# Attention scores of a hybrid mixer: 288 rows of high and low parts in two full passes and one on row quarters

## The chip, the cores and the metric

One Trainium2 chip, one of its NeuronCores. The metric is the device time of one execution in microseconds. A change is compared by the median of repeated runs. All arithmetic that counts is float32; products that must be nearly exact in float32 are made from a high part (the value rounded to the float32r type) and a low part (value minus high part), as high x high + high x low + low x high.

## What is computed

A transformer layer over 2048 tokens (x) and 256 context tokens, width 1024, in the order of the reference:

```
h, hc = modulated rmsnorm of x, ctx
cq, ckv, kr, rq, rk, rv, rg = split(h @ w_in)
q = (rmsnorm(cq) @ w_uq)      8 heads x (64 plain + 32 rope)
k, v = rmsnorm(ckv) @ w_ukv   8 heads x 64; the 32 rope rows of k are shared by all heads
s = q . k * 96**-0.5 ; p = softmax(s over 2304 keys) ; o = p @ v
y = [o, bidirectional retention of rq, rk, rv gated by rg] @ w_o
x = x + ga1 * y ; then a 16-expert feed-forward on the normed x, and a final rmsnorm
```

The change is about s, the scores: 2048 queries x 2304 keys x 8 heads over 96 rows (64 plain, 32 rope).

## The kernel before, in words

The program runs stages one after the other, each in a block of its own with all five engines in step by semaphores. Every engine executes its own instruction list in order; `sg[name].wait(engine, turn, k)` makes it wait for the k-th increment of that turn.

**project** (18 turns of 128 tokens). TensorE multiplies the normed tokens by w_in in high and low parts (L501), transposes the latents (L526), and makes q (L542), k (L548), v (L554), the chunk state (L560) and q transposed per head (L568). VectorE does norms, the sums of the rest of the modulation (L723), rope for the retention keys (L707 to L714), h^T (L692, L694), latent_T (L764) and the rope rows of the attention key, kr_T (L765); TensorE's L542 waits for the last increment of `latT`, which L765 gives. At the end of its turn VectorE waits for ScalarE's statistics (L586). SyncE stores k, q, kr and the rest to scratch in device memory, in a fixed order (L418).

**retention** (16 chunks). Among others the 128 x 128 scores of eight heads are made by L968 on 64 rows of the array each: four heads on rows 0 to 63, then four heads on rows 64 to 127.

**attention** (L1178 to L1462), the stage that the change rewrites. The work is 32 blocks: 8 heads x 4 blocks of 512 queries. SyncE loads a head's k^T and q^T (96 rows: 64 plain, 32 rope) two heads ahead; ScalarE rounds them (L1355) and VectorE subtracts (L1394), in thirds between blocks. For every key tile of 128 keys (18 of them) three passes of 96 rows and 512 columns add into one of four PSUM banks:

```
for n, (kp, qp) in enumerate(((0, 0), (0, 1), (1, 0))):
    m = pe.matmul(banks[S_BANKS[kt % 4]][:, :], kT[u][:, kp, k], qT[u][:, qp, q], ...)
```

A turn of TensorE is: all 54 score passes of block b+1, then six groups of `weighted` of block b (three key tiles each: values times probabilities on 64-column halves of the array, L1315, and the sums of the probabilities on 32-column quarters, L1319), with the transposes that find the maximum of block b+1 between them (`max_rows` L1297 after group 2, `max_spread` L1305 after group 4). ScalarE copies each score tile out of PSUM (L1360, 512 columns each) and takes the exponentials of three tiles at a time (L1365). VectorE takes the maximum over keys (L1402, L1405, L1411, L1416, L1418), subtracts it (`shift`, L1424), inverts the sums (L1430) and multiplies the outputs by the inverse (L1435, eight small instructions), before SyncE stores them to `attT`.

**mix_out** (16 tiles of 128 tokens): loads the attention output (L1521), ScalarE rounds it (L1628), GpSimd takes the low part (L1560), TensorE multiplies by w_o (L1585), VectorE adds, norms and routes. **experts** follows and is not changed but for the semaphores that it takes over.

## Time and profile before

| | us |
|---|---|
| median of 3 runs (2973.39 to 2991.9) | 2974.0 |
| the profiled execution, its own time | 2979.84 |
| its span in the trace | 2978.0 |
| TensorE matmul busy, of the span | 2749.8 (92%) |
| VectorE busy | 2099.8 (71%) |
| ScalarE busy | 1441.5 (48%) |
| GpSimd busy | 348.9 (12%) |
| the L1285 score passes, busy | 413.9 |

Durations below are of the one profiled execution. In its rows a group has its busy time, its count and the mean of one instruction; matmuls overlap in the pipeline, so the mean of one (400 ns for a score pass) is longer than the distance from one to the next. A time of one step is therefore taken from the start of a group of instructions to the start of the next one. In the trace a matmul on plain float32 operands appears as two instructions, one on float32r as one. "PEld" is the load of the stationary operand, which stands in the trace as an engine of its own.

### The profile page before, as it was taken

How to read it: one execution, taken by the hardware profiler on the slowest of the kernel's cores; microseconds unless marked ns; L12 is line 12 of the kernel's file. 1: busy time of each engine (PE TensorE's matmuls, PEld its weight loads, DVE VectorE, ACT ScalarE, POOL GpSimd, SP SyncE). 2: the span in 40 equal slices, each digit the busy share in tenths (PEclk: the TensorE clock that was granted, in tenths of full speed). 3: DMA queues.
4: the chain of work that ended last, by engine and by line, in shares of the span. 5: the costliest groups of instructions: out<-in, count | busy, mean ns of one | idle time of the engine just before them, and what ended most of it. 6: DMA issues, size and time to landing. Idle time of an engine off the chain costs nothing. (4 is left out here: it accounts for less than half of the span.)

```text
span 2978.0 us, 57085 instructions
## 1 busy us (share of the span) xinstructions
PE 2749.8 (92%) x20805; PEld 2244.1 (75%) x20805; DVE 2099.8 (71%) x3131; ACT 1441.5 (48%) x2146; POOL 348.9 (12%) x377
## 2 busy tenths in 40 slices
PE   5999999899959999999999979992999999999996
PEld 2877777688847766766766748882989988988995
DVE  3555554677749999999999965547667667657666
ACT  3555555322237767767766742112444444444444
POOL 0111111222210000000000002210101101101102
PEclk8999999999979999999999989995999999999998
DMA  7544443422230110110110024334667767767778
GB/s 244 176 158 151 149 149 113 134 76 76 62 61 3 37 33 10 37 32 11 37 34 10 5 85 153 134 116 132 206 191 226 225 190 207 226 179 219 226 217 306
DMA packets 267042, 375.33 MB, mean 126 GB/s; under 512 B 35571, under 2 KB 186646, under 8 KB 265174
## 3 DMA queue, kind: packets, MB, share of 16 engines
q1 hardware_dynamic: 257334, 337.83, 35.5%
q0 software_dynamic: 9504, 34.61, 5.0%
q8 instruction: 150, 2.46, 0.4%
q14 instruction: 54, 0.44, 0.1%
HBM read 286.61 MB, written 85.77 MB: 125 GB/s over the span
## 5 line engine op out<-in xcount | busy, mean ns | idle before, releaser
L2012 PE MATMUL ebank<-gathered_T,w_gate_up 128*128 128x256 f32 x4608 | 552.5, 282 | 20.8 <-issue 13.8
L2012 PEld LDWEIGHTS ebank<-gathered_T,w_gate_up 128*128 128x128 f32 x4608 | 548.3, 190 | 24.3 <-issue 23.4
L1285 PE MATMUL abank<-head_qT,head_kT 96*128 96x512 f32 x1728 | 413.9, 400 | 22.8 <-DVE head_qT L1394 17.0
L1285 PEld LDWEIGHTS abank<-head_qT,head_kT 96*128 96x128 f32 x1728 | 325.6, 191 | 104.2 <-issue 29.3
L1365 ACT ACTIVATE scores<-scores 128x1536 f32<-128x1536 f32 x192 | 274.3, 1476 | 232.9 <-DVE scores L1424 232.9
L1424 DVE TENSOR_TENSOR scores<-scores,abank 128x1536 f32<-128x1536 f32 x192 | 322.6, 1747 | 47.9 <-PE abank L1305 44.8
L1360 ACT ACTIVATE scores<-abank 128x512 f32<-128x512 f32 x576 | 325.4, 601 | 41.7 <-PE abank L1285 16.0
L501 PE MATMUL bank<-w_in_sb,h_T 128*128 128x512 f32 (+1 forms) x1296 | 292.5, 384 | 9.1 <-DVE h_T L702 9.1
L1315 PE MATMUL abank<-scores,head_v 128*64 128x256 f32 x2304 | 291.0, 388 | 1.2 <-ACT scores L1365 1.2
L2026 PE MATMUL ebank<-w_down,hidden_T 128*128 128x512 f32 x1152 | 281.1, 399 | 3.5 <-DVE w_down L2244 3.4
L501 PEld LDWEIGHTS bank<-w_in_sb,h_T 128*128 128x128 f32 x1296 | 243.7, 190 | 44.0 <-DVE h_T L702 7.2
L2026 PEld LDWEIGHTS ebank<-w_down,hidden_T 128*128 128x128 f32 x1152 | 212.6, 188 | 53.3 <-issue 6.0
L1405 DVE TENSOR_TENSOR score_max<-score_max,scores 128x1536 f32<-128x1536 f32 x128 | 225.0, 1758 | 7.7 <-ACT scores L1360 1.1
L2239 DVE TENSOR_TENSOR w_gate_up<-w_gate_up_whole,w_gate_up 128x2048 fp32r<-128x2048 f32 x96 | 215.4, 2285 | 13.5 <-ACT w_gate_up L2054 13.5
L1315 PEld LDWEIGHTS abank<-scores,head_v 128*64 128x64 f32 x2304 | 148.2, 136 | 97.6 <-issue 39.7
L1585 PE MATMUL obank<-w_o_sb,mix_tile 128*128 128x512 f32 x768 | 183.9, 396 | 20.4 <-DVE w_o_sb L1702 20.4
L2054 ACT ACTIVATE w_gate_up<-w_gate_up_whole 128x2048 fp32r<-128x2048 f32 x96 | 178.1, 1905 | 45.4 <-DMA w_gate_up_whole<-in_w_exp_up 45.4
L2073 ACT ACTIVATE gate_exp<-ebank 128x256 f32<-128x256 f32 x96 | 36.8, 383 | 328.6 <-PE ebank L2012 328.5
L1585 PEld LDWEIGHTS obank<-w_o_sb,mix_tile 128*128 128x128 f32 x768 | 143.5, 190 | 49.4 <-issue 20.6
L933 PE MATMUL rbank<-w_query_gate_hi,chunk_h_T 128*128 128x512 f32 x512 | 167.7, 399 | 13.8 <-DVE w_query_gate_lo L1069 13.8
L1319 PEld LDWEIGHTS abank<-scores,head_v 128*32 128x32 f32 x4608 | 114.1, 109 | 73.9 <-issue 73.9
L1319 PE MATMUL abank<-scores,head_v 128*32 128x128 f32 x4608 | 165.6, 277 | 0.0
(285 smaller groups left out, 3637.0 us busy)
## 6 DMA issues: line engine op xcount, KB each, us to landing
w_gate_up_whole<-in_w_exp_gate SPq DMA_DIRECT2D x48, 1024.0 KB, 5.4
w_gate_up_whole<-in_w_exp_up SPq DMA_DIRECT2D x48, 1024.0 KB, 9.0
w_down_whole<-in_w_exp_down SPq DMA_DIRECT2D x192, 256.0 KB, 5.8
ada_rest<-in_w_ada SPq DMA_DIRECT2D x16, 1024.0 KB
x_tile<-in_x_all SPq DMA_DIRECT2D x18, 512.0 KB
scratch_h<-h_T_whole SPq DMA_DIRECT2D x18, 512.0 KB, 2.7
ada_w<-in_w_ada SPq DMA_DIRECT2D x4, 2048.0 KB
chunk_h_T_whole<-scratch_h SPq DMA_DIRECT2D x16, 512.0 KB
```

Source lines behind the costliest of these rows:

```text
L501: m = pe.matmul(banks[bank][:, 0:n], hT[u][:, hp, k, :], w_in[:, wp, k, lo:lo + n], start=(k == 0 and i == 0), stop=(k == KD - 1 and i == 2))
L1285: m = pe.matmul(banks[S_BANKS[kt % 4]][:, :], kT[u][:, kp, k], qT[u][:, qp, q], start=(n == 0), stop=(n == 2))
L1315: pe.matmul(ps[64 * half:64 * half + 64, 0:HB], v1[u][:, kt, 0:DV], p[:, kt, half * HB:(half + 1) * HB], start=(kt == 0), stop=(kt == T - ...
L1319: m = pe.matmul(ps[32 * c:32 * c + 32, HB:HB + P], v1[u][:, kt, DV:DV + 32], p[:, kt, c * P:(c + 1) * P], start=False, stop=(kt == T - 1), ...
L1360: act.activation(sc[j % 2][:, kt, :], banks[S_BANKS[kt % 4]][:, :], ACT.Copy).then_inc(sg["scores"].sem, 1)
L1365: act.activation(x, x, ACT.Exp, scale=ATT_SCALE).then_inc(sg["probs"].sem, 1)
L1405: dve.tensor_tensor(mx[:, :, :], mx[:, :, :], s[:, g * G:(g + 1) * G, :], ALU.max).then_inc(sg["max_keys"].sem, 1)
L1424: dve.tensor_tensor(x, x, mid(banks[4][:, :], G), ALU.subtract).then_inc(sg["shifted"].sem, 1)
L1585: x = pe.matmul(banks[2 * u + half][:, :], mt[u][:, mp, k, :], w_o[:, wp, k, half * 512:(half + 1) * 512], start=(k == 0 and n == 0), stop ...
L2012: x = pe.matmul(banks[f % 3][:, j * CAP:(j + 1) * CAP], w_gu[c][:, wp, j, k, o:o + P], xsT[:, xp, k, :], start=(k == 0 and n == 0), stop=( ...
L2026: x = pe.matmul(banks[Y_BANKS[2 * c + h]][:, :], hid[:, hp, k, h * P:(h + 1) * P], w_d[i % RING][:, wp, :], start=(k == 0 and n == 0), sto ...
L2239: dve.tensor_tensor(w_gu[c][:, 1, j], w_gu_whole[c][:, 1, j], w_gu[c][:, 0, j].bitcast(F32), ALU.subtract).then_inc(sg["gu_rest"].sem, 1)
```

## The change

1. **Parts are made once, in project.** ScalarE's copies out of PSUM now round (k, q), and VectorE subtracts (`low_parts`, at the end of its turn, and one 32 x 128 subtraction for the rope rows of k behind L765). High and low parts are stored, so the stores of k, q and kr double in size. The splits inside attention (L1355, L1394) are gone. The `latT` signal has five increments, the last by the new subtraction.
2. **Stacked scores.** The three products of 64 + 32 rows are 288 rows. Two passes of 128 rows take 256 of them (k_hi with q_hi, all 96 rows, and the 32 rope rows of k_hi with q_lo; then the plain rows of k_hi with q_lo and of k_lo with q_hi). The last 32 rows (rope of k_lo with q_hi) run as one matmul of 32 rows on row quarter `kt % 4` of the array. A score group is three key tiles: six full passes, then three quarter passes.
3. **Order of a block.** TensorE interleaves the groups: scores 0, 1, weighted 0, scores 2, 3, weighted 1, scores 4, 5, weighted 2 to 4, `max_rows`, weighted 5, `max_spread`. Score banks are six (two groups of three); ScalarE copies three tiles by one instruction of 1536 columns. All six shifts follow `max_spread`; before, two of them stood in the turn before.
4. **Loads by GpSimd.** A head's stacked operands are seven loads (3.87 MB; before 1.67 MB in three loads from SyncE's queue), the rope quarters of q four loads of 64 KB for each block. Before the first score pass stand the seven loads of head 0, four of rope q, and eight of the rope rows of k.
5. **Division moved.** ScalarE copies the undivided output (`out_rows`), VectorE inverts the sums as before and SyncE stores them; mix_out loads them broadcast to the rows (two loads for each tile) and VectorE multiplies (`scale_att`), one instruction of 128 x 512 for each tile, at the end of its turn.
6. **Retention scores** alternate between the two 64-row halves.
7. Bookkeeping: scale and shift of h^T are read from `modcols`, two staging buffers are gone, the modulation bias is loaded later in SyncE's turn, semaphores are reused.

Core of the diff:

```diff
@@ project, SyncE, GpSimd, VectorE
-                store(t, "latT", krT[:, :], scratch["kT"][4, 0:ROPE, at], "kr_stored")
+                store(t, "latT", krT[:, :, :].bitcast(F32), scratch["kr"][:, :, at].rearrange("s d n -> d s n"), "kr_stored")
...
+                if queries and ahead == 2:
+                    sg["mod_stored"].wait(sp, t - TC)
+                    settled(sp)
+                    load_bias(t * MW + 2 * D, u)
+                store(t, "k_lo", k_sb[:, :, :, :].bitcast(F32), ..., "k_stored")
...
+            def low_parts(t, queries):
+                sg["k_rows"].wait(dve, t)
+                dve.tensor_tensor(k_sb[:, 1, :, :], banks[6]..., k_sb[:, 0, :, :].bitcast(F32), ALU.subtract).then_inc(sg["k_lo"].sem, 1)
+                if queries:
+                    for g in range(2):
+                        sg["qT_rows"].wait(dve, t - TC, g + 1)
+                        dve.tensor_tensor(qT_sb[:, 1, h, :], banks[5 + 2 * g][0:DQ, :]..., ALU.subtract).then_inc(sg["q_lo"].sem, 1)
...
-                dve.tensor_copy(krT[:, :], banks[2][0:ROPE, 3 * P:4 * P]).then_inc(sg["latT"].sem, 1)
+                dve.tensor_copy(krT[:, 0, :], kr_ps).then_inc(sg["latT"].sem, 1)
+                sg["latT"].wait(dve, t, 4)
+                dve.tensor_tensor(krT[:, 1, :], kr_ps, krT[:, 0, :].bitcast(F32), ALU.subtract).then_inc(sg["latT"].sem, 1)
                 if ahead:
                     rest(t + 1, 1 - u)
+                low_parts(t, queries)
@@ retention, TensorE
-                for par in range(2):
-                    f = slice(64 * par, 64 * par + 64)
-                    for a in range(4):
+                for a in range(4):
+                    for par in range(2):
+                        f = slice(64 * par, 64 * par + 64)
@@ attention, TensorE
+            def scores(u, nq, b, g):
+                sg["scores"].wait(pe, b if g >= 2 else b - 1, g - 1 if g >= 2 else g + GROUPS - 1)
+                for kt in range(g * G, (g + 1) * G):
+                    k, ps = slice(kt * P, (kt + 1) * P), s_ps[:, kt % (2 * G), :]
+                    pe.matmul(ps, ka[u][:, k], qa[u][:, q], start=True, stop=False)
+                    pe.matmul(ps, kb[u][:, k], qb[u][:, q], start=False, stop=False)
+                for kt in range(g * G, (g + 1) * G):
+                    r = slice(kt % 4 * R4, kt % 4 * R4 + R4)
+                    m = pe.matmul(s_ps[:, kt % (2 * G), :], kc[r, kt // 4, :], qc[r, nq % 2, :], start=False, stop=True)
+                m.then_inc(sg["s_psum"].sem, 1)
@@ attention, GpSimd
+            load_kq(0, 0)
+            load_qc(0, 0, 0)
+            load_kr()
@@ mix_out, VectorE
+            def scale_att(m, u):
+                att_loaded.wait(dve, m, u)
+                x = mt_whole[u][:, 1, 0:KH, :]
+                dve.tensor_tensor(x, x, inv[u][:, :, :], ALU.mult).then_inc(sg["att_scaled"].sem, 1)
```

How the order moves on TensorE in the attention loop. Names are output<-inputs (abank: the PSUM banks; a count of 6 or 12 float32 matmuls stands for 12 or 24 instructions of the trace). Before, the last score passes of block b+1 and the start of the weighted groups of block b:

```order
L1285 MATMUL abank<-head_qT,head_kT 128x512 x3
L58 REGISTER_ALU
L1285 MATMUL abank<-head_qT,head_kT 128x512 x3
L58 ISA x2
L1315 MATMUL abank<-scores,head_v 64x256 x6
L1319 MATMUL abank<-scores,head_v 32x128 x12
L58 REGISTER_ALU
```

Now, the end of one score group and the one weighted group before the next scores (L1330 and L1331 are the two full passes, L1334 the three quarter passes, L1358 and L1362 the weighted group):

```order
L1330 MATMUL scores_ps<-head_q_hi,head_k_hi 128x512
L1331 MATMUL scores_ps<-head_q_lo_hi,head_k_hi_lo 128x512
L1334 MATMUL scores_ps<-rope_q_hi,rope_k_lo 128x512 x3
L58 REGISTER_ALU
L1358 MATMUL out_ps<-scores,head_v 64x256 x6
L1362 MATMUL out_ps<-scores,head_v 32x128 x12
L58 REGISTER_ALU
L1330 MATMUL scores_ps<-head_q_hi,head_k_hi 128x512
```

A block has six such changes from full passes to quarter passes, and its scores stand in three places instead of one.

On VectorE in project, the end of a turn and the start of the next; before:

```order
L764 TENSOR_SCALAR latent_T<-bank,shared_cols 128x128 x3
L765 COPY kr_T<-bank 32x128
L702 TENSOR_TENSOR h_T<-h_T_whole,h_T 128x512 x2
L731 TENSOR_TENSOR chunk_state<-chunk_state,decay_chunk 64x512
L733 TENSOR_TENSOR chunk_state<-chunk_state,bank 64x512
```

Now:

```order
L779 TENSOR_SCALAR latent_T<-bank,shared_cols 128x128 x3
L781 CAST kr_T<-bank 32x128
L783 TENSOR_TENSOR kr_T<-bank,kr_T 32x128
L706 TENSOR_TENSOR h_T<-h_T_whole,h_T 128x512 x2
L733 TENSOR_TENSOR kT_rows<-bank,kT_rows 128x512
L738 TENSOR_TENSOR qT_rows<-bank,qT_rows 96x512 x2
L746 TENSOR_TENSOR chunk_state<-chunk_state,decay_chunk 64x512
L748 TENSOR_TENSOR chunk_state<-chunk_state,bank 64x512
```

One subtraction is added ahead of the signal for which TensorE's q product waits, and three behind it, which wait for ScalarE's copies of this turn.

## Rows read from the trace of the kernel before

**Rows 1.** Stretches: us, busy PE, PEld, DVE, ACT, POOL (counts), clock, DMA share, GB/s

```profile
100.00:500.00 400.00, 384.68 (x1979) 312.18 (x1978) 217.55 (x481) 222.69 (x410) 74.09 (x92) 1.00 0.46 153
600.00:820.00 220.00, 220.00 (x1385) 191.79 (x1384) 170.08 (x204) 57.07 (x95) 63.63 (x60) 1.00 0.24 72
868.27:1764.00 895.73, 880.20 (x8896) 615.50 (x8896) 814.03 (x802) 616.74 (x810) 0.00 (x0) 0.99 0.10 23
```

**Rows 2.** Timeline of TensorE over one attention block: start, duration, line, count

```profile
918.78 12.65 PE L1285 MATMUL abank<-head_qT,head_kT 96*128 96x512 f32 x54
931.37 1.52 PE L1315 MATMUL abank<-scores,head_v 128*64 128x256 f32 x12
...
945.97 12.69 PE L1285 MATMUL abank<-head_qT,head_kT 96*128 96x512 f32 x54
```

**Rows 3.** Timeline of TensorE around the retention scores

```profile
705.65 0.39 PE L933 MATMUL rbank<-w_query_gate_hi,chunk_h_T 128*128 128x512 f32 x1
705.97 1.71 PE L968 MATMUL rbank<-chunk_qT,chunk_kT 64*128 64x128 f32 x16
707.61 0.66 PE L986 MATMUL rbank<-ident,y_out 128*128 128x128 f32 x4
```

**Rows 4.** L968 alone, instructions that touch each stretch (TensorE, PEld)

```profile
705.97:706.51 0.54, 0.54 (x4) 0.54 (x5) 1.00 0.00 0
706.51:706.96 0.45, 0.45 (x10) 0.45 (x9) 1.00 0.00 0
```

**Rows 5.** Timeline of TensorE in mix_out: the 16-column router product

```profile
1840.96 1.86 PE L1602 MATMUL obank<-w_router_sb,h_T 128*128 128x16 f32 x16
1842.66 5.71 PE L1585 MATMUL obank<-w_o_sb,mix_tile 128*128 128x512 f32 x24
```

**Rows 6.** Timeline of ScalarE and VectorE in one attention block

```profile
945.51 8.40 DVE L1424 TENSOR_TENSOR scores<-scores,abank 128x1536 f32<-128x1536 f32 x5
954.31 4.99 ACT L1360 ACTIVATE scores<-abank 128x512 f32<-128x512 f32 x9
955.62 7.14 DVE L1405 TENSOR_TENSOR score_max<-score_max,scores 128x1536 f32<-128x1536 f32 x4
959.19 5.59 ACT L1365 ACTIVATE scores<-scores 128x1536 f32<-128x1536 f32 x4
964.12 0.95 DVE L1430 RECIPROCAL sums_inverse<-abank 128x128 f32<-128x128 f32 x1
965.11 2.38 DVE L1435 TENSOR_TENSOR out_T<-abank,sums_inverse 32x128 f32<-32x128 f32 x8
```

**Rows 7.** Timeline of a project turn

```profile
337.74 0.27 DVE L765 COPY kr_T<-bank 32x128 f32<-32x128 f32 x1
338.14 2.84 PE L542 MATMUL bank<-w_uq_sb,latent_T 128*128 128x384 f32 x8 [0.24 <-DVE kr_T L765]
345.12 1.08 ACT L639 ACTIVATE qT_rows<-bank 96x512 f32<-96x512 f32 x2
350.47 0.75 DVE L682 TENSOR_SCALAR x_normed<-x_tile,x_stats 128x1024 f32<-128x1024 f32 x1 [9.20 <-ACT x_stats L586]
```

**Rows 8.** Start of attention: timeline, then stretches (columns as rows 1)

```profile
852.13 1.15 SPq L1248 DMA_DIRECT2D head_kT_whole<-scratch_kT  x2
868.27 14.71 PE L1285 MATMUL abank<-head_qT,head_kT 96*128 96x512 f32 x54 [17.02 <-DVE head_qT L1394]
856.00:862.00 6.00, 0.00 (x0) 0.00 (x0) 0.00 (x0) 0.00 (x0) 0.00 (x0) 0.50 1.00 209
```

**Rows 9.** Groups of GpSimd's own transfers (busy, mean ns of one)

```profile
L1945 POOL DMA_INDIRECT scratch_acc<-expert_out,slot_tokens x30 | 70.4, 2348 | 558.4 <-DVE expert_out L2263 553.8 <-issue 4.6
```

**Rows 10.** Timeline of mix_out: its start, and a later turn of VectorE

```profile
1769.83 0.98 SPq L1521 DMA_DIRECT2D mix_tile_whole<-scratch_attT  x2
1783.62 23.98 PE L1585 MATMUL obank<-w_o_sb,mix_tile 128*128 128x512 f32 x96 [20.41 <-DVE w_o_sb L1702]
...
1848.41 0.69 DVE L1681 TENSOR_TENSOR x_tile<-obank,ga_rows 128x512 f32<-128x512 f32 x1 [4.91 <-PE obank L1585]
```

More of the change, by code:

```diff
@@ L705, in rope_ret @@
                 src = halves(banks[bank][:, :])
-                a, b = (halves(rterm[:, j, :]) for j in range(2))
+                a, b = halves(dst), halves(rterm[:, :])
+                stored.wait(dve, t - 1)
                 dve.scalar_tensor_tensor(a, src, scale, mid(cos_r[:, u, :], H), ALU.mult, ALU.mult).then_inc(sig.sem, 1)
@@ L1269, in _ @@
             loop(sp, turn)
+            sg["sums_stored"].wait(sp, BLOCKS - 1)
             sg["out_stored"].wait(sp, BLOCKS - 1)
@@ L1274, in _, with turn @@
+            load_kq(0, 0)
+            load_qc(0, 0, 0)
+            load_kr()
             for u in range(2):
                 pool.memset(v1[u][:, :, DV:], 1.0).then_inc(ones_set, 1)
+            load_qc(0, QB, 1)
+            load_kq(1, 1)
+            sg["s_psum"].wait(pool, 0)
+            load_qc(0, 2 * QB, 0)
+            def turn(pair, j, b, more):
+                if not more:
+                    return
+                sg["s_psum"].wait(pool, b + 1)
+                settled(pool)
+                nxt = j + 3
+                if nxt < 2 * NB or not isinstance(pair, int):
+                    load_qc(pair * 2 + nxt // NB, nxt % NB * QB, (j + 1) % 2)
+                if j % NB == NB - 2 and not isinstance(pair, int):
+                    load_kq(pair * 2 + (2 + j // NB), j // NB)
@@ L1277, in _ @@
+            loop(pool, turn)
         @block.tensor
         def _(pe):
-            def score(u, qb, b, kt):
-                q = slice(qb * QB, (qb + 1) * QB)
-                k = slice(kt * P, (kt + 1) * P)
-                sg["scores"].wait(pe, b, kt - 3 if kt > 3 else min(kt - 1, 0))
-                for n, (kp, qp) in enumerate(((0, 0), (0, 1), (1, 0))):
-                    m = pe.matmul(banks[S_BANKS[kt % 4]][:, :], kT[u][:, kp, k], qT[u][:, qp, q], start=(n == 0), stop=(n == 2))
-                m.then_inc(sg["s_psum"].sem, 1)
@@ L1325, in turn, with next_scores @@
                 u, nu = j // NB % 2, nxt // NB % 2
+                def next_scores(g):
+                    if more:
+                        scores(nu, nxt, b + 1, g)
                 if more:
                     if nxt % NB == 0:
-                        head_ready(pair * 2 + 1 if nxt == NB else pair * 2 + 2, nu)
-                    for kt in range(T):
-                        score(nu, nxt % NB, b + 1, kt)
-                for g in range(GROUPS):
-                    m = weighted(u, j, b, g)
-                    if more and g == 2:
-                        max_rows(b + 1)
-                    if more and g == 4:
-                        max_spread(b + 1)
-                m.then_inc(sg["out_psum"].sem, 1)
-            sg["rounded"].wait(pe, 0)
-            sg["rest"].wait(pe, 0)
-            for kt in range(T):
-                score(0, 0, 0, kt)
+                        head = pair * 2 + 1 if nxt == NB else pair * 2 + 2
+                        kq_loaded.wait(pe, head, nu)
+                        v_loaded.wait(pe, head, nu)
+                    qc_loaded.wait(pe, b + 1, nxt % 2)
+                next_scores(0)
+                next_scores(1)
+                weighted(u, j, b, 0)
+                next_scores(2)
+                next_scores(3)
+                weighted(u, j, b, 1)
+                next_scores(4)
+                next_scores(5)
+                for g in (2, 3, 4):
+                    weighted(u, j, b, g)
+                if more:
+                    max_rows(b + 1)
+                weighted(u, j, b, 5).then_inc(sg["out_psum"].sem, 1)
+                if more:
+                    max_spread(b + 1)
+            kq_loaded.wait(pe, 0, 0)
+            qc_loaded.wait(pe, 0, 0)
+            pe.wait_ge(kc_loaded, 8 * 32)
+            for g in range(GROUPS):
+                scores(0, 0, 0, g)
             max_rows(0)
@@ L1389, in _ @@
         def _(dve):
[L1390 to L1394 removed]
             def maximum(j, b, g):
                 s = sc[j % 2]
[L1399 removed]
+                sg["scores"].wait(dve, b, g + 1)
                 if g == 1:
@@ L1445, in turn @@
                     fold(b + 1)
-                if j:
-                    output(j - 1, b - 1)
-                if more:
                     spread(b + 1)
-                    split_next(split, pair, j)
-                    for g in (0, 1):
-                        shift((j + 1) % 2, b + 1, g)
                 if j == 2 * NB - 1:
-                    output(j, b)
-            for n in range(3):
-                split(0, 0, n)
+                    inverse_sums(b)
             for g in range(1, GROUPS):
@@ L1697, in turn @@
                     probabilities(m - 2)
+                if ahead:
+                    scale_att(m + 2, u)
+            for u in range(2):
+                scale_att(u, u)
             for n in range(4):
```

333 lines of the change are left out of this document (169 added, 164 removed).

## The prediction

> **What bounds the kernel now.** I read first the page's busy slices and its sums: TensorE is busy in 92% of the span, so an edit on another engine pays only where TensorE waits for it. Then the stretches of the stages [rows 1]: TensorE is busy for 384.68 of 400.00 us in project, for all of 220.00 in retention and for 880.20 of 895.73 in attention, at the full clock (0.99 to 1.00, the level of 2.4 GHz). VectorE has 814.03 in attention, 91%: it is close behind. Then the timeline of one block [rows 2]: the 54 score passes start at 918.78, the weighted groups at 931.37, the next scores at 945.97. A block is 27.19 us: 12.59 for scores (0.23 us a pass) and 14.60 for six weighted groups and two sets of transposes, without a gap. So attention is a sum of TensorE's work, and the question is what the new passes cost in place, with what they make the array change over to. The last thing I read is the start of the stage [rows 8], where TensorE stands still for 17.02 us behind loads and splits.
>
> **A score group.** The number of passes falls from 54 to 36 full ones and 18 on quarters. If three quarter passes run side by side they cost one, and 54 passes become 42. But the array must change from full rows to quarters and back six times in a block. The trace has such a change in retention [rows 3]: the last full pass of 512 columns starts at 705.65 and the first on 64 rows at 705.97, 0.32 us later where a pass to the next is 0.23. So 0.09 is lost, and the weight load is not hidden behind the pass before any more. What a load of 128 columns takes by itself the router product shows, where only 16 columns are multiplied [rows 5]: 16 instructions in 1.70 us, 0.106 each.
>
> Do the row parts run side by side? The 16 instructions of L968 show it where the first half's last ones meet the second half's first [rows 4]: 4 matmuls touch the first 0.54 us, 10 touch the next 0.45 us, which at one after the other every 0.11 us (each lasting some 0.27) would be 6 or 7; and the loads are as many (5, then 9), so loads for two row parts run side by side too. All 16 take 1.64 us [rows 3], less than 16 x 0.106 = 1.70.
>
> A group is then: exposed load 0.11, five steps between full passes 5 x 0.23 = 1.15, last full pass to the next load 0.32, exposed load 0.11, three quarter passes together and the change back 0.32: 2.01 us. Six make 12.06 against 12.59. The transposes of `max_spread` now stand before full passes and need no change of shape, some 0.1. The weighted groups cost the same wherever they stand, since their changes to other shapes are in the 14.60 already. A block becomes 27.19 - 0.53 - 0.10 = 26.56 us; 31 blocks: **-19.5 us**.
>
> The Trainium skill, "TensorEngine Tiling (Array Packing)", Key Properties, states that a change of tiling mode drains the engine; the 0.09 and the exposed load are what the trace has of it. The skill, "TensorE: Matmul & The Clock Gate", Part 3, gives 3.07 times for four 32-row tiles of 512 columns instead of 4; by that the three passes would take some 0.07 us longer, an estimate, and the change would be worth 12 us less.
>
> **Do the other engines keep up?** From `max_spread` the first shift takes 1.68 (8.40 for five [rows 6]) and the first exponential 1.4 (5.59 for four); with hand-overs 4.0 us after it starts. TensorE meanwhile has the transposes and two score groups, 4.5. ScalarE copies three tiles at once: nine tiles took 4.99, so three some 1.4 to 1.66; with six copies, six exponentials and the output its block is 17.7 to 19. VectorE runs six shifts (10.1), the inversion (0.95), five maxima (4 in 7.14, so 8.9), folds and spread: about 24, and it loses the 2.38 of L1435 and the splits. Of that, the folds end some 22.1 us after `max_spread` starts; TensorE comes to `max_rows` after the transposes, six score groups and five weighted ones of 2.24 (14.60 less two sets of 0.6, by six): 0.5 + 12.06 + 11.2 = 23.8. So TensorE stays the bound by 1.7 us: faster passes would meet VectorE.
>
> **Start of attention.** Before: first load 852.13, first pass 868.27 [rows 8], with loads moving 209 GB/s and the first head's splits behind them. Now seven loads (3.87 MB), rope q 0.26 and the rope rows of k 1.47 must land: 5.6 MB, 27 us at that rate; with the two v loads in SyncE's queue beside them (1.18 MB) 32 us. With 2 us to start, the first pass is at 881 to 886, against 868: +13 to +18. Lower bound: at twice the rate +1; upper bound: 19 issues by GpSimd at the 2.35 of its indirect ones [rows 9] are 45 us, +31. I take **+15**. The skill, "DMA: Bandwidth & Descriptors", Measured, has 341 GB/s for 1 MB transfers issued from GpSimd; by that the first pass would be at 870 to 874. Loads of later heads have more than four blocks (100 us) for 3.87 MB, and are hidden; so are the rope quarters, asked for over one turn ahead.
>
> **Project.** The new subtraction on 32 x 128 stands between kr_T (0.27) and L542, and TensorE already waited 0.24 there [rows 7]: +0.3 a turn, 18 turns, **+5** (bounds 0, if what follows absorbs it, to 8). The three behind it (2.1 us) start when ScalarE's copies end (346.20 [rows 7]) and end by 347.6, where VectorE idled 9.20 us until 350.47: nothing. SyncE's additional wait (`mod_stored`) stands before the k store, whose low part comes later anyway; nobody needs these stores in the turn. The doubled stores add 0.7 MB to a turn of 26 us, DMA share 0.46 to about 0.55: nothing, at worst +5 if h_T's store lands later.
>
> **Retention.** With the halves alternating, 16 instructions become 8 steps of 0.11 plus entry and exit 0.2: 1.1 instead of 1.64 [rows 3], 16 chunks, **-9** (bounds 0, and -12), as TensorE has no gap there.
>
> **mix_out and the seams.** Four more loads are issued before w_o, 0.49 each [rows 10], and 0.5 MB lands first: TensorE's start at 1783.62 moves by **+2**. The multiplication at a turn's end (0.7) and its wait for the loads fall into VectorE's 4.91 us idle; ScalarE's rounding is for two tiles ahead. Cover gone, it would cost 0.7 x 16 = 11. The tail of attention loses L1435, **-2**.
>
> **Sum.** -19.5 + 15 + 5 - 9 + 2 - 2 = -8.5. On the profiled execution 2979.84 gives 2971; it lay 6 us above the median of the runs, so against 2974.0 I forecast **2966**. A measurement tells about 1% (30 us) from no change; this is below it.
>
> **Rivals.**
> 1. *Slower: the quarters don't overlap.* Only two halves in one place speak for overlap, in float32 and 128 columns; here three quarters write three banks that full passes have just written. If the three run in turn, a group is 2.01 + 2 x 0.23 = 2.47, a block +2.8, +86 us; with retention's gain gone too, 3060. If only their weight loads come in turn (2 x 0.106), a block is +1.3, +39: 3006. The change is slower than before from a group of 2.1 us plus the start. Against it: the equal counts of loads and matmuls in rows 4. Chance 0.17.
> 2. *Faster: no change-over between full rows and quarters* (quarters aren't halves; weights may be loaded behind). A group is 7 x 0.23 = 1.61; TensorE's block would be 24.2, but `max_rows` then waits for the folds at 22.1; with it (0.6) and the last weighted group (2.24) behind it the block is 25.0. That is -2.2 x 31 = -68, less the other terms: 2917. Halfway, a group of 1.8, gives 2928. Against it: rows 3. Chance 0.23.
> 3. *The loads decide.* GpSimd's issues at 2.35 us, or slower transfers, put the first pass at 897 or later, or its queue delays a head: 2980 to 3000, no change that can be told. Chance 0.15.
> 4. The forecast, 0.45.
>
> **How the numbers follow.** Faster by over 1% (below 2944): rival 2 and a little of the forecast's spread, 0.24. Slower (above 3004): rival 1 and the far end of rival 3, 0.19. The rest 0.57. The likeliest case alone spans 2950 to 2985; the range 2917 to 3006 takes rival 2 and rival 1's milder form.
>
> **What would show it.** Right: in the timeline of a block, 0.32 from the last full pass to the quarters, three quarters counted within some 10 ns of each other, and groups 2.0 us apart; a block of 26.6; VectorE idle about 1.7 us before its first shift; first pass of attention near 884; L968's successor at 1.1 us; L542 idle 0.5 instead of 0.24. Wrong: quarters 0.23 apart (rival 1), a full pass within 0.23 of the quarters (rival 2), TensorE waiting for ScalarE's copies or for a first exponential, or a block above 27.2.

## The result and the profile after

The changed kernel takes 3055.62 us (median, 3053.59 to 3058.42), the kernel before 2979.91 in the same series: a ratio of 1.0251, 95% interval 1.0227 to 1.0275. It is slower by some 76 us; I had forecast no change that can be told, 2966 us, in a range of 2917 to 3006. The profiled execution spans 3056.7 us against 2978.0.

A sum like this one is read by cutting both spans at the same places of the program. These are the cuts in the timelines of the kernel before that the sections ahead don't show: the first pass of retention, its last transposes, the last sums of attention, the first work on the router's choice, the experts' first product.

```profile
537.41 0.77 PE L933 MATMUL rbank<-w_query_gate_hi,chunk_h_T 128*128 128x512 f32 x1 [13.75 <-DVE w_query_gate_lo L1069]
...
850.13 1.11 PE L986 MATMUL rbank<-ident,y_out 128*128 128x128 f32 x4 [5.99 <-DVE y_out L1134]
...
1762.36 0.86 PE L1319 MATMUL abank<-scores,head_v 128*32 128x128 f32 x24
...
2013.13 0.69 PE L1968 MATMUL ebank<-ident,affinities_by_half 128*128 128x128 f32 x2 [1.76 <-DVE affinities_by_half L2160]
...
2077.03 13.40 PE L2012 MATMUL ebank<-gathered_T,w_gate_up 128*128 128x256 f32 x96 [1.69 <-DVE gathered_T L2234]
```

And the same places after, with the first score pass [rows 8] and the first product with w_o [rows 10]:

```profile
545.58 0.77 PE L952 MATMUL rbank<-w_query_gate_hi,chunk_h_T 128*128 128x512 f32 x1 [15.40 <-DVE w_query_gate_lo L1089]
...
852.07 1.11 PE L1006 MATMUL rbank<-ident,y_out 128*128 128x128 f32 x4 [5.99 <-DVE y_out L1154]
...
886.76 0.77 PE L1330 MATMUL scores_ps<-head_q_hi,head_k_hi 128*128 128x512 f32 x1 [33.58 <-DMA rope_k_lo<-scratch_kr]
...
1759.59 0.86 PE L1362 MATMUL out_ps<-scores,head_v 128*32 128x128 f32 x24
1790.44 23.85 PE L1625 MATMUL obank<-w_o_sb,mix_tile 128*128 128x512 f32 x96 [29.98 <-DVE w_o_sb L1752]
...
2065.07 0.69 PE L2014 MATMUL ebank<-ident,affinities_by_half 128*128 128x128 f32 x2 [1.75 <-DVE affinities_by_half L2206]
...
2128.39 13.20 PE L2058 MATMUL ebank<-gathered_T,w_gate_up 128*128 128x256 f32 x96 [1.69 <-DVE gathered_T L2280]
```

| stretch | before | after | difference | forecast |
|---|---|---|---|---|
| to the first pass of retention | 537.4 | 545.6 | +8.2 | +5 |
| retention | 312.7 | 306.5 | -6.2 | -9 |
| to the first score pass | 18.1 | 34.7 | +16.5 | +15 |
| attention blocks | 894.1 | 872.8 | -21.3 | -19.5 |
| to the first product with w_o | 21.3 | 30.9 | +9.6 | 0 (+2 - 2) |
| mix_out | 229.5 | 274.6 | **+45.1** | 0 |
| choice and gather | 63.9 | 63.3 | -0.6 | 0 |
| experts to the end | 901.0 | 928.3 | **+27.3** | 0 |

The forecast's -2 for the tail of attention stands in the row of w_o, since L1435 runs behind the last sums. The start of attention and its blocks come out within 2 us of the forecast. What makes the kernel slower lies behind them, above all in two stages whose products are the same as before. The table's first row, up to retention, is the least steady: in two more traces of programs with the stages of before (e4 and e10 below) the first pass of retention comes at 540.2 and 540.5, and in those of the changed kernel's variants e1, e2, e3, e6 and e12 at 543.5 to 546.6.

Three rows for the stretches, first the attention blocks, then mix_out to its last product, then the experts (columns as [rows 1]):

```profile
886.76:1760.40 873.64, 858.34 (x8896) 530.92 (x8896) 706.09 (x511) 548.98 (x415) 80.36 (x162) 0.99 0.25 50
1790.44:2053.00 262.56, 231.01 (x1112) 193.42 (x1112) 123.99 (x166) 42.92 (x92) 58.32 (x60) 0.92 0.44 127
2128.39:3056.70 928.31, 866.10 (x6480) 807.48 (x6480) 604.38 (x1050) 393.73 (x576) 116.45 (x75) 0.96 0.69 210
```

In mix_out's stretch TensorE stands still for 31.6 us and its granted clock falls from 0.99 to 0.92. The kernel before has there

```profile
1783.62:2001.00 217.38, 215.16 (x1112) 183.08 (x1112) 110.48 (x152) 42.89 (x92) 51.63 (x60) 0.99 0.41 140
2077.03:2978.00 900.97, 856.95 (x6480) 798.95 (x6480) 604.31 (x1050) 393.91 (x576) 115.78 (x75) 0.98 0.71 216
```

**Attention.** TensorE's timeline of one block, from one `max_spread` to the next:

```profile
961.77 0.66 PE L1347 MATMUL max_ps<-ident,score_max 128*128 128x128 f32 x4
...
963.41 0.40 PE L1331 MATMUL scores_ps<-head_q_lo_hi,head_k_hi_lo 128*128 128x512 f32 x1
963.74 0.50 PE L1334 MATMUL scores_ps<-rope_q_hi,rope_k_lo 32*128 32x512 f32 x3
964.17 0.50 PE L1330 MATMUL scores_ps<-head_q_hi,head_k_hi 128*128 128x512 f32 x1
964.51 0.40 PE L1331 MATMUL scores_ps<-head_q_lo_hi,head_k_hi_lo 128*128 128x512 f32 x1
...
966.19 1.52 PE L1358 MATMUL out_ps<-scores,head_v 128*64 128x256 f32 x12
...
988.29 0.66 PE L1347 MATMUL max_ps<-ident,score_max 128*128 128x128 f32 x4
```

The three quarter passes together take 0.50 us, and each of them lasts 0.49 to 0.50 by itself, so they start nearly at once. They start 0.33 after the last full pass, and the next full pass follows 0.43 later. A group is 966.19 - 964.17 = 2.02 us (forecast 2.01), a block 988.29 - 961.77 = 26.52 us (forecast 26.56).

**mix_out.** Timelines of TensorE, then VectorE's multiplication, then SyncE's loads of the same turn:

```profile
1849.73 1.03 PE L1634 MATMUL obank<-ident,x_normed 128*128 128x128 f32 x8
1854.94 7.35 PE L1625 MATMUL obank<-w_o_sb,mix_tile 128*128 128x512 f32 x24 [4.18 <-POOL mix_tile L1600]
...
1870.17 5.72 PE L1625 MATMUL obank<-w_o_sb,mix_tile 128*128 128x512 f32 x24
```

```profile
1849.69 0.69 DVE L1699 TENSOR_TENSOR mix_tile_whole<-mix_tile_whole,inverse_sums 128x512 f32<-128x512 f32 x1 [5.82 <-DMA inverse_sums<-scratch_inverse]
```

```profile
1855.02 0.57 SPq L1559 DMA_DIRECT2D mix_tile_whole<-scratch_attT  x1
1855.68 1.43 SPq L1561 DMA_DIRECT2D inverse_sums<-scratch_inverse  x2
```

and the whole stage in the list of waits (total, times, longest):

```profile
DVE mix_tile_whole L1699 <- DMA inverse_sums<-scratch_inverse: 98.9, 16, 14.8
ACT mix_tile L1668 <- DVE mix_tile_whole L1699: 142.5, 13, 16.6
```

VectorE waits 16 times for the inverse sums, some 5.6 us in a turn after the first. They are asked for behind the mix tile, which is asked for only after the turn's residual (the sum of x and the product, which ends in `x_tile`), and are used some 9 us after their issue (1855.68, multiplied at 1864.74). The multiplication is the last thing in VectorE's turn, and the next turn's residual is queued behind it: residual, store and three loads, landing, multiplication, next residual is a ring of 16.5 us a turn (TensorE's second gap of the kind ends at 1887.85, two tiles and 32.9 us behind the one at 1854.94), where TensorE's own turn is 13.6. TensorE stands still on every second tile, and the granted clock falls behind the gap: 24 products take 7.35 us there, at a mean clock of 0.76, and 5.72 elsewhere.

```profile
1854.94:1862.10 7.16, 7.16 (x24) 5.74 (x25) 2.82 (x4) 0.15 (x2) 0.79 (x2) 0.76 0.78 196
```

The stage has seven such gaps of 3.25 to 6.67 us, 29.3 together, and the 24 products behind each take 7.16 to 8.49 us, 14.2 more together than at full clock. That is 43.4 of the stage's 45.1 us.

The margin that this used up stands in the timelines before: GpSimd's low part was ready at 1831.40 + 1.30, and TensorE began the products that follow it at 1835.41, 2.7 us later.

```profile
1831.40 1.30 POOL L1560 TENSOR_TENSOR mix_tile<-ret_mix_T,mix_tile 128x512 fp32r<-128x512 f32 x1
...
1835.41 5.71 PE L1585 MATMUL obank<-w_o_sb,mix_tile 128*128 128x512 f32 x24
```

**Experts.** No instruction of the experts' loop was changed. TensorE's timeline at a return of its loop, of the kernel before and then of the changed one:

```profile
2404.91 13.02 PE L2012 MATMUL ebank<-gathered_T,w_gate_up 128*128 128x256 f32 x96 [3.47 <-issue]
```

```profile
2240.17 0.62 PE L2058 MATMUL ebank<-gathered_T,w_gate_up 128*128 128x256 f32 x3 [3.68 <-DVE w_gate_up L2285]
2244.49 5.71 PE L2058 MATMUL ebank<-gathered_T,w_gate_up 128*128 128x256 f32 x33 [3.70 <-issue]
```

Before, TensorE stands still once, 3.5 us, waiting for nothing that the profile shows; so it does at five of the six returns, one of them put down to ScalarE (5.3 us). After, it stands still, makes three products, and stands still again, at each of the six. The profile puts the first of the two waits down to VectorE at three of them, as in the row above, and to nothing at the other three. The mean granted clock around the second wait is 0.53 (a stretch of the changed kernel):

```profile
2241.00:2248.00 7.00, 3.51 (x17) 3.51 (x17) 4.74 (x19) 1.64 (x1) 2.48 (x2) 0.53 0.93 169
```

Loads on the instruction queue stand beside it, in pieces of 16 KB (0.74 MB in 45 packets). The profile doesn't say for which engine (packets, MB, share; 2240 to 2816 us of the changed kernel):

```profile
q8 instruction: 45, 0.74, 0.5%
```

So two theories stood against their rivals. **A:** mix_out loses its time by the inverse sums' landing inside VectorE's ring; rival **B:** any multiplication or wait at that place would do it. **C:** the experts lose theirs because the instructions ahead of the loop became fewer and its head moved against the 16 KB pieces; rival **D:** memory traffic or the clock that the stage begins with.

### The profile page after: what moved, and what is told of

The parts are those of the page before. It is cut to its first block and busy times, and to the rows that moved or that the text cites. A ratio compares the mean times of both kernels' runs of the same rounds, so it can differ in the third digit from the quotient of the medians.

```text
span 3056.7 us, 56434 instructions
## 1 busy us (share of the span) xinstructions
PE 2747.9 (90%) x20805; PEld 2170.7 (71%) x20805; DVE 2040.3 (67%) x2907; ACT 1369.6 (45%) x1746; POOL 452.4 (15%) x569
## 5 line engine op out<-in xcount | busy, mean ns | idle before, releaser
L2058 PEld LDWEIGHTS ebank<-gathered_T,w_gate_up 128*128 128x128 f32 x4608 | 556.8, 193 | 44.2 <-issue 30.9
L1478 DVE TENSOR_TENSOR scores<-scores,max_ps 128x1536 f32<-128x1536 f32 x192 | 322.9, 1738 | 48.1 <-PE max_ps L1347 48.1
L1413 ACT ACTIVATE scores<-scores_ps 128x1536 f32<-128x1536 f32 x192 | 275.0, 1447 | 132.2 <-PE scores_ps L1334 132.2
L1358 PE MATMUL out_ps<-scores,head_v 128*64 128x256 f32 x2304 | 293.0, 390 | 3.9 <-ACT scores L1418 3.9
L1330 PE MATMUL scores_ps<-head_q_hi,head_k_hi 128*128 128x512 f32 x576 | 248.8, 432 | 38.9 <-DMA rope_k_lo<-scratch_kr 33.6
L1625 PE MATMUL obank<-w_o_sb,mix_tile 128*128 128x512 f32 x768 | 198.0, 418 | 59.2 <-DVE w_o_sb L1752 30.0
L1331 PE MATMUL scores_ps<-head_q_lo_hi,head_k_hi_lo 128*128 128x512 f32 x576 | 229.2, 398 | 0.0
L2285 DVE TENSOR_TENSOR w_gate_up<-w_gate_up_whole,w_gate_up 128x2048 fp32r<-128x2048 f32 x96 | 215.4, 2285 | 13.6 <-ACT w_gate_up L2100 13.6
L1358 PEld LDWEIGHTS out_ps<-scores,head_v 128*64 128x64 f32 x2304 | 149.4, 137 | 102.0 <-issue 46.8
L1625 PEld LDWEIGHTS obank<-w_o_sb,mix_tile 128*128 128x128 f32 x768 | 153.6, 203 | 93.7 <-issue 57.0
L1330 PEld LDWEIGHTS scores_ps<-head_q_hi,head_k_hi 128*128 128x128 f32 x576 | 109.4, 190 | 93.4 <-issue 70.9
L1271 POOL DMA_DIRECT2D rope_q_hi<-scratch_q x128 | 63.0, 499 | 725.8 <-PE scores_ps L1334 720.8
```

The costliest lines, as they stand in the source:

```text
L1330: pe.matmul(ps, ka[u][:, k], qa[u][:, q], start=True, stop=False)
L1331: pe.matmul(ps, kb[u][:, k], qb[u][:, q], start=False, stop=False)
L1358: pe.matmul(o_ps[64 * half:64 * half + 64, 0:HB], v1[u][:, kt, 0:DV], p[:, kt, half * HB:(half + 1) * HB], start=(kt == 0), stop=(kt == T ...
L1413: act.activation(sc[j % 2][:, g * G:(g + 1) * G, :], s_ps[:, g % 2 * G:g % 2 * G + G, :], ACT.Copy).then_inc(sg["scores"].sem, 1)
L1478: dve.tensor_tensor(x, x, mid(m_ps[:, :], G), ALU.subtract).then_inc(sg["shifted"].sem, 1)
L1625: x = pe.matmul(banks[2 * u + half][:, :], mt[u][:, mp, k, :], w_o[:, wp, k, half * 512:(half + 1) * 512], start=(k == 0 and n == 0), stop ...
```

## The experiments

**e1_inverse_early.** The inverse sums of a tile are asked for before the wait for the residual.

```diff
             def turn(m, u, behind, ahead):
+                if ahead:
+                    sg["att_scaled"].wait(sp, m)
+                    settled(sp)
+                    load_inv(m * P + 2 * P, u)
                 sg["x2"].wait(sp, m)
```

> Theory A (mix_out loses its time because the inverse sums, two broadcast loads behind the load of the mix tile, land 9 us after the residual of the turn, and VectorE waits for them at the end of its turn with the next turn behind it): here the inverse sums of a tile are asked for before the wait for the residual, about 8 us earlier; the wait at the turn's end then ends with the mix tile's own load, some 5 us after its issue, and TensorE's gaps of 3.3 to 6.7 us on every second tile go. mix_out from its first product to the affinities' transposes 230 us instead of 274.6; the whole -40 to -46, about 3012. Rival B (the wait's place in VectorE's turn, or the multiplication itself, is what costs, whatever lands): gaps stay, above 3040. The experts' stage is unchanged in both (928 us).

Measured: 3015.86 us, ratio to before 1.0123 (1.0076 to 1.0170); from the first product to the affinities' transposes 232.0 us instead of 274.6. In the 14 turns of the loop the wait that is left is the mix tile's own, 9.4 us in all; the inverse sums are waited for only at the two multiplications ahead of w_o (the view of the tile of inverse sums). The stage runs at full clock:

```profile
  DMA inverse_sums<-scratch_inverse: 21.5, 2
  DMA mix_tile_whole<-scratch_attT: 9.4, 14
```

```profile
1793.82:2014.00 220.18, 216.54 (x1112) 183.80 (x1112) 120.35 (x166) 43.17 (x93) 51.81 (x61) 0.99 0.50 151
```

The experts kept their 928.6 us. Theory A holds for the stage: the multiplication and a wait stand where they stood, and only the request moved. The seam ahead of w_o keeps its loss (TensorE idle 30.85 us there).

**e2_no_inverse_loads.** No inverse sums are loaded; VectorE multiplies by ones at the same place. The kernel leaves the division out, so only its time counts.

```diff
-                for w in range(2):
-                    sp.dma_start(inv[u][64 * w:64 * w + 64, :, :], scratch["inverse"]...partition_broadcast(64))...
...
+            for u in range(2):
+                pool.memset(inv[u][:, :, :], 1.0).then_inc(power_set, 1)
```

> Leaves the division out: no inverse sums are loaded, the mix tile is multiplied by ones at the same place of VectorE's turn and waits only for its own load. Theory A: as with the early loads, no gap in mix_out, and the start of mix_out some 3 us earlier besides, since nothing is queued ahead of the weights: about 3008 to 3012. Rival B: the gaps stay, above 3040. Between the two (3020 to 3035): both the wait's place and the landing matter.

Measured: 3002.87, ratio 1.0077 (1.0054 to 1.0101); mix_out 230.1 us. TensorE's idle time ahead of w_o is back at 19.41 us (after 29.98, before 20.41 [rows 10]):

```profile
1778.89 24.08 PE L1625 MATMUL obank<-w_o_sb,mix_tile 128*128 128x512 f32 x96 [19.41 <-DVE w_o_sb L1753]
```

So the two pairs of broadcast loads that stand ahead of w_o are the +9.6 at the seam. I had expected 3 us of them here; it is 10.6. This run alone leaves open whether w_o lands later or VectorE's wait holds up its split of w_o. The traces tell: ScalarE's rounding of the first piece of w_o, which waits for its landing, before and then after, and VectorE's second multiplication after:

```profile
1779.24 1.91 ACT L1647 ACTIVATE w_o_sb<-w_o_sb_whole 128x2048 fp32r<-128x2048 f32 x1 [4.03 <-DMA w_o_sb_whole<-in_w_o]
```

```profile
1786.06 1.91 ACT L1687 ACTIVATE w_o_sb<-w_o_sb_whole 128x2048 fp32r<-128x2048 f32 x1 [7.37 <-DMA w_o_sb_whole<-in_w_o]
1783.05 0.69 DVE L1699 TENSOR_TENSOR mix_tile_whole<-mix_tile_whole,inverse_sums 128x512 f32<-128x512 f32 x1 [5.62 <-DMA inverse_sums<-scratch_inverse]
```

The loads of w_o start to be issued at 1770.85 before and 1770.84 after, so the first piece is used 8.4 us later before and 15.2 after (7.9 without the inverse sums). VectorE is free at 1783.74, ahead of it: the landing of w_o sets the start.

**e3_pad32.** Instructions that do nothing for the result, on TensorE's queue.

```diff
+            for _ in range(32):
+                settled(pe)
             loop(pe, turn)
```

> The changed kernel with 32 increments of a semaphore on TensorE's queue ahead of the loop of experts, which move the loop's head by 32 instructions. Theory C (the 27 us that the experts' stage lost come from the instruction loads of 16 KB, 256 instructions of 64 bytes: the head of TensorE's loop now lies a few instructions ahead of a block's end, so two blocks are waited for at each return, with 3 products between them, and the clock falls): one wait of some 3.5 us at a return instead of two, a pair of experts 111 us instead of 115, the whole -20 to -28, about 3030. Rival D (the stage is slower through DMA traffic, memory layout or the state of the clock that it enters with): no change, 3050 to 3060.

Measured: 3009.48, ratio 1.0110 (1.0064 to 1.0157), -46 us, where theory C had asked for -20 to -28. The stretch of the experts and TensorE's timeline at the same return of the loop:

```profile
2128.35:3001.80 873.45, 849.43 (x6480) 793.52 (x6480) 600.57 (x1049) 390.90 (x574) 116.26 (x75) 0.99 0.73 222
```

```profile
2232.64 3.90 PE L2072 MATMUL ebank<-w_down,hidden_T 128*128 128x512 f32 x16
2236.38 11.37 PE L2058 MATMUL ebank<-gathered_T,w_gate_up 128*128 128x256 f32 x96
```

There is no wait at this return or any other, and between 2220 and 2870 us not one load on that queue. The stage is 55 us shorter than after and 27 shorter than before.

**e4_before_pad165.** The same line with 165 in the kernel before, so that its loop starts 256 instructions behind the changed kernel's (number 9408 in TensorE's program against 9152, a product counted as two; the kernel before has 9243).

> The kernel before with 165 increments of a semaphore on TensorE's queue ahead of the loop of experts, so that the loop's head stands at the same place of a 256-instruction block as in the changed kernel. Theory C: two waits at each return with 3 products between them, experts' stage 926 instead of 901, the whole +20 to +28, about 3002. Rival D: only the increments' own time, at most 5 us, if it isn't hidden: 2974 to 2985.

Measured: 3031.60, ratio 1.0178 (1.0131 to 1.0225). Of the 52 us, 24.71 are the increments themselves, ahead of the first product; I had taken 5 at most. Most of the rest is the stage, 925.24 us instead of 900.97, and the double wait is there, with three products between:

```profile
2103.46 12.74 PE L2012 MATMUL ebank<-gathered_T,w_gate_up 128*128 128x256 f32 x96 [24.71 <-issue]
2214.57 0.62 PE L2012 MATMUL ebank<-gathered_T,w_gate_up 128*128 128x256 f32 x3 [3.42 <-issue]
2218.65 12.67 PE L2012 MATMUL ebank<-gathered_T,w_gate_up 128*128 128x256 f32 x93 [3.46 <-issue]
```

Rival D is out: the kernel before, with its own data and loads, gets 24.3 of the changed kernel's 27.3 us by position.

**e9_best.** e1's edit, 32 increments ahead of the wait for the gathered rows, and two edits of order: the second mix tile and its inverse sums are loaded behind w_o (and multiplied behind w_o's splits), and head_v behind the first head's keys and queries.

```diff
-            load_att(P, 1)
...
+            kq_loaded.wait(sp, 0, 0)
+            settled(sp)
             for u in range(2):
                 load_v(u, u)
```

> The changed kernel with four edits: inverse sums asked for before the residual (-42 as measured), the loop's head of the experts moved by 32 instructions at a place where TensorE waits anyway (-55 in the stage as measured, one pair of experts 104 us, no instruction loads in the loop), the first mix tile and its inverse sums loaded ahead of w_o and the second behind it with its multiplication behind w_o's splits (from the last weighted pass to the first product of mix_out 22 us instead of 30), and head_v loaded behind the first head's keys and queries (first score pass 6 us earlier). Sum -42 -55 -8 -6: about 2945, and below both kernels. If the effects overlap, for instance when the clock's halves are counted twice, 2955 to 2965.

Measured: 2959.98, ratio 0.9921 (0.9893 to 0.9949), faster than both kernels. But the two edits of order gave little. TensorE's idle time ahead of w_o is 23.74 instead of 29.98, and gaps of 2.75 and 3.28 us came in front of the second and third tiles, with mix_out at 238.7 instead of e1's 232.0, so nothing is left of it. The first score pass came after 31.43 us of idle time instead of 33.58 (33.0 to 35.5 in the seven traces with the old order), some 2 us and not 6.

**e10_before_pad195.** The kernel before, 9 increments in each of the 15 rounds of the search and 60 behind the first `slots`, where TensorE waits anyway.

> The kernel before with 195 increments of a semaphore on TensorE's queue at places where it waits ahead of the loop of experts, so that the loop's head stands at the same place of an instruction block as in e3_pad32. Theory C, in the form that the loop of 1748 instructions stays loaded when it touches 7 blocks of 256 and not when it touches 8: no instruction load between the second and the last pair, the stage 874 us instead of 901, the whole 2950 to 2955. If the attention change had left something behind that e3_pad32 only undid, no gain: 2975 to 2985.

Measured: 2956.44, ratio 0.9913 (0.9888 to 0.9938); the stage 873.7 us, no load on the instruction queue between 2175 and 2820. What e3 gained has nothing to do with the attention change.

**e5_same_quarter.** The three 32-row passes of a group all read rows 0 to 31.

```diff
-                    r = slice(kt % 4 * R4, kt % 4 * R4 + R4)
+                    r = slice(0, R4)
```

> All three passes of 32 rows of a group read the same quarter of rows (the low part of the rope rows is then that of one tile for all three, so the scores lack their own low part). Theory O (passes on different quarters run side by side and cost one together): here they are 0.23 us apart, a group is 2.0 + 0.46 = 2.5 us, a block 29.3 instead of 26.5, 31 blocks +85 us, about 3140. Rival (the three merely follow one another quickly because each is short, wherever they stand): group 2.0 and no change, 3056.

Measured: 3156.26 in a single run. TensorE's timeline of a group:

```profile
964.86 0.39 PE L1331 MATMUL scores_ps<-head_q_lo_hi,head_k_hi_lo 128*128 128x512 f32 x1
965.18 0.96 PE L1334 MATMUL scores_ps<-rope_q_hi,rope_k_lo 32*128 32x512 f32 x3
966.07 0.51 PE L1330 MATMUL scores_ps<-head_q_hi,head_k_hi 128*128 128x512 f32 x1
```

The three take 0.96 us instead of 0.50, 0.46 more in each of 192 groups, 88 of the 100 us that this run is longer. From the first quarter pass to the next full pass it is 0.89 instead of 0.43. Passes on different quarters run side by side.

**e6_halves_in_turn.** Retention's score products in the order of before.

```diff
-                for a in range(4):
-                    for par in range(2):
+                for par in range(2):
+                    for a in range(4):
```

> The score products of retention back in the order of before, one half of the rows after the other. If the alternation is worth what their own time shows (16 instructions 1.16 us instead of 1.71), the stage is 0.55 x 16 = 9 us longer, from 306.5 to 315 us; if only what the stage as a whole showed against before, 6 us, 312.7. The score products: 1.7 us for 16 in both.

Measured: 3063.18 in a single run. Sixteen take 1.71 us again (timeline), and retention, from 545.00 to 860.13, is 315.1 us:

```profile
733.74 1.71 PE L987 MATMUL rbank<-chunk_qT,chunk_kT 64*128 64x128 f32 x16
```

The alternation is worth 8.6 us, as its own time says.

**e11_start_and_seam.** As e9_best, with fewer bytes ahead of the first pass, and with the second mix tile and its inverse sums loaded between the halves of w_o (not in this cut of the edit).

```diff
-            load_kq(0, 0)
+            load_kq(0, 0, slice(0, QB))
             load_qc(0, 0, 0)
-            load_kr()
+            load_kr(0)
+            load_kc()
...
+            sg["s_psum"].wait(pool, 0, 1)
+            settled(pool)
+            load_q(0, 0, kc_loaded, slice(QB, SEQ))
+            load_kr(1)
             load_kq(1, 1)
```

> As e9_best, with the start of attention cut to what the first block needs: of the first head's queries only the 512 columns of the first block, the rope rows of the keys for one buffer set only, the rest and the second head behind the first group of scores; the second mix tile and its inverse sums between the halves of w_o. If the start is the time that the loads take (5.6 MB at some 215 GB/s before the first pass, 3.4 MB now), the first pass comes 10 us earlier, near 876; if it is the number of issues on GpSimd (17 of them at 0.5 us) it comes at most 2 us earlier. Second mix tile 2 to 4 us. Together about 2947, below e10_before_pad195 (2956); by the second reading 2956.

Measured: 2947.52 (2946.70 to 2950.35), ratio 0.9899 (0.9858 to 0.9941). The first pass (timeline):

```profile
874.13 0.77 PE L1342 MATMUL scores_ps<-head_q_hi,head_k_hi 128*128 128x512 f32 x1 [20.10 <-DMA rope_k_lo<-scratch_kr]
```

TensorE waits 20.10 us for it instead of 31.43. GpSimd issues 17 loads ahead of it instead of 19, at some 0.5 us each, and 3.4 MB instead of 5.6: two issues are about 1 us, so bytes and not issues set the start. The gap ahead of the second mix tile only moved (3.92 us, now between the halves of the first).

**e12_pad80.** The changed kernel with 80 increments behind the first `slots`.

> The changed kernel with 80 increments ahead of the loop of experts at a place where TensorE waits, so that the loop's 1748 instructions begin some 72 behind a block's start and touch 8 blocks of 256 again, but with the head's block long enough for the first products. Theory C (whether all of the loop stays loaded is set by 7 or 8 blocks): blocks are loaded again in every pair, with one wait of some 3.5 us at a return as in the kernel before, stage 895 to 905 us. If any move away from the place just ahead of a border were enough (only the double wait counts), no loads in the loop and 874 us as in e3_pad32.

Measured: 3017.35 in a single run; the stage 880.80 us, one return with loads, 9 of them between 2230 and 2885 us:

```profile
q8 instruction: 9, 0.15, 0.1%
```

Neither form of theory C fits: it is neither every pair nor none. The positions together (number of the loop's first instruction in TensorE's program, counted as for e4, less full 256s):

| kernel | position | loads on the queue (stretch) | stage, us |
|---|---|---|---|
| after / e4 | 192 / 192 | 45 (576 us) / 45 (576) | 928.3 / 925.2 |
| e3 / e10 | 224 / 222 | 0 (650 us) / 0 (645) | 873.5 / 873.7 |
| e12 | 16 | 9 (655 us) | 880.8 |
| before | 27 | 36 (553 us) | 901.0 |

Two different programs agree at the same position less 256s (192, and 224 with 222), and the stage grows with the loads. Only TensorE's program was shifted in e3, e4, e10 and e12, and the loads changed with it, so they are taken to be TensorE's. The Trainium skill, "Runtime: NRT & Kernel Launch", Instruction fetch mechanics, says that instructions come in blocks of 16 KB, 256 of them, that TensorE has room for 2048, and that a taken branch to a block that isn't there waits for it. The pieces of 16 KB and the period of 256 agree with these runs. The page also speaks of a window of two blocks; there the runs disagree, since a loop of 1748 instructions went round for 650 us without a load. By that room, an estimate from the page's 2048, a loop that touches seven blocks has one to spare and one that touches eight has none. No run here shows where a block's border is, so the reading by seven and eight blocks is argued and not shown, and why one of the six returns waits at position 16, five at 27 and all at 192 stays open. What is shown is that the position sets the stage's time.

## Why the prediction was wrong

**mix_out, the step that failed.** The forecast said that the multiplication and its wait "fall into VectorE's 4.91 us idle", and priced the case without cover at 0.7 x 16 = 11. It priced the instruction and put the wait at nothing; measured, the stage was 45.1 us longer, with VectorE waiting 98.9 us in all for the inverse sums. An idle time at the head of a turn is cover for work that is ready; a wait for a landing that is itself released by the same turn closes a ring. The trace of before had the numbers: from the end of the residual to the low part's end 9.5 us (1823.18 to 1832.70), with 2.7 to spare, and the change put two broadcast loads and the multiplication into that chain. e1 takes 42.6 of the 45.1 away by moving the request, and nothing else. None of the forecast's rivals was this one, nor the experts' loss below.

**The seam, mis-sized.** +2 for "four more loads" and 0.5 MB, and -2 for the tail of attention; it was +9.6, and without the loads (e2) TensorE's idle time is 1.0 below before. The loads were counted by their issue times and bytes; with them ahead of w_o, its first piece was used 15.2 us after its issue instead of 8.4. The tail gained 0.5 and not 2: mix_out's first load is issued 6.51 us after the last sums begin instead of 7.02. Whether it is the loads' place in the queue or their pieces that delays w_o, no run separates.

**Not in the sum: code position.** The forecast took stages that the change doesn't touch as unchanged. The changed TensorE program is 91 instructions shorter ahead of the experts, and that cost 27.3 us, as e3 and e4 show from both sides (e4 gives 24.3 of it to the kernel before by position alone). The rows that would have warned were in the trace of before: waits of 3.3 to 3.5 us "<-issue" at returns of the loop, with loads on the instruction queue. A stall that depends on position can go either way with any edit: the stage here took from 27 us less than before to 27 more, and the range should have had room for both.

**Right, with runs for it.** The group: 2.01 forecast, 2.02 measured, with 0.33 and 0.43 to and from the quarters, and a block of 26.52; e5 excludes rival 1 and the timeline rival 2. The start: +15 forecast, +16.5 measured, by transfer rate (the first pass at 886.76 against a forecast of 881 to 886); e11 confirms that it is the bytes. Retention's alternation: -9 forecast, 8.6 by e6; the stage shows only -6.2, because with the old order in the changed kernel it is 2.4 us longer than in the kernel before, which no run explains. Project: +5 forecast for TensorE's wait behind kr_T; that wait went from 5.7 to 12.8 us in all, and the stage from 537.4 to 545.6, or by 6 us between the means of all the traces named above.

Without the +45.1, the +27.3 and the seam's +9.6, the table adds up to -3 us, where the forecast was -8.5. So the rest of the change is worth next to nothing either way here: 21 us won in the blocks and 6 in retention are spent at the start of attention (16.5) and in project (8). With the loop of the experts in the same favourable position, the kernel before takes 2956.44 and e11, which also mends start and mix_out, 2947.52; their ratios to before (0.9888 to 0.9938 and 0.9858 to 0.9941) overlap, so it is not shown that the changed scores win anything over the old ones.

## What to carry to other kernels

When work moves to a later stage, draw that stage's ring: which wait releases the request, when it lands, and what is queued behind the one who waits for it. Ask for what depends on nothing first. And before believing a small difference, compare the stages that were not changed; if a loop shows waits "<-issue" at its return and loads on the instruction queue, shift its start by a few dozen instructions and measure both kernels so.

## What the runs showed of the hardware

- A stage whose TensorE loop has 1748 instructions took 873 to 928 us for the same products, by where the loop starts (e3, e10, e12, before, e4, after); 32 increments of a semaphore ahead of it won 55 us in the stage (e3).
- An increment on TensorE's queue cost 24.71 / 165 = 0.15 us where nothing hid it (e4).
- In mix_out after the change, each of the seven gaps of 3.25 to 6.67 us on TensorE was followed by products partly at the lower of its two clock levels (1.2 instead of 2.4 GHz; mean granted clock 0.76 behind the gap at 1854.94): 24 of them took 7.16 to 8.49 us instead of 5.72, so a gap cost 1.4 to 2.8 us more than its length. The extra cost differs from gap to gap: in the experts of before, 96 products that usually take 11.37 us took 11.57 behind a gap of 3.53 us and 13.95 behind one of 3.45.
- Three passes of 512 columns on three different quarters of the rows took 0.50 us, on the same quarter 0.96 (e5).
- Two broadcast loads of 128 KB from device memory, asked for behind a tile of 256 KB, were used 9 us after their issue (after); in e1, the tile without them behind it was used 4.7 us after its own (1850.73 to 1855.38).
